# The last expert round moved into the next block, and one expert matrix fetched ahead

## The reference

```python
scores = sigmoid(x @ w_router); idx = grouped top-8 of 64 experts; wsel = 2.5 * normalised scores
routed = sum over the 8 chosen experts e of wsel[e] * (silu(x @ w_gate[e]) * (x @ w_up[e])) @ w_down[e]
x = x + g2 * (routed + swiglu(x, shared weights))
h = rmsnorm(x) * gain * (1 + scale) + shift      # the next layer's input; after layer 1: the final norm
```

## Time and profile before

| | |
|---|---|
| median of 3 runs | 1618.62 us (1614.11 to 1620.0) |
| profiled execution | 1614.77 us, its span 1613.0 us, mean TensorE clock 0.987 |
| TensorE matmuls busy | 1516.2 us, 94% of the span |
| VectorE, ScalarE, GpSimd busy | 709.3, 364.3, 94.0 us |
| moved by DMA | 580.21 MB, 360 GB/s in the mean, 420 GB/s in the expert rounds |

### The profile page before, as it was taken

How to read it: one execution, slowest core, us unless ns; L and a number is a source line. 1 busy time by engine, 2 the same in 40 slices (tenths; PEclk the granted TensorE clock), 3 DMA queues, 4 the chain that set the end, 5 groups by cost and what they waited for, 6 DMA issues and landing times. The chain is left out here.

```text
span 1613.0 us, 29632 instructions
## 1 busy us (share of the span) xinstructions
PE 1516.2 (94%) x11206; PEld 1009.5 (63%) x11206; DVE 709.3 (44%) x1980; ACT 364.3 (23%) x770; POOL 94.0 (6%) x119
## 2 busy tenths in 40 slices
PE   6999999998999999999997799999999999999986
PEld 4778765776665665565554487767566556565553
DVE  3205535215465355345454235443745534543453
ACT  3002443103111121112111244431111111211112
POOL 0000110001000000000000000001000000010000
PEclk9999999999999999999999899999999999999998
DMA  9997799339999999999999793988999999999896
GB/s 364 388 370 266 259 394 404 124 98 367 393 420 420 420 421 420 419 420 419 398 370 409 265 291 110 351 305 325 420 420 421 421 420 420 420 419 410 338 420 248
DMA packets 153578, 580.21 MB, mean 360 GB/s; under 512 B 17181, under 2 KB 62401, under 8 KB 105226
## 3 DMA queue, kind: packets, MB, share of 16 engines
q1 hardware_dynamic: 137642, 535.74, 83.8%
q0 software_dynamic: 15200, 40.92, 6.6%
q10 hardware_dynamic: 640, 2.26, 0.4%
HBM read 567.17 MB, written 26.90 MB: 368 GB/s over the span
## 5 line engine op out<-in xcount | busy, mean ns | idle before, releaser
L2431 PE MATMUL ps<-ring,scratch 128*64 128x256 f32 x3328 | 367.8, 380 | 10.0 <-DMA ring<-in_moe_w_up 8.8
L2431 PEld LDWEIGHTS ps<-ring,scratch 128*64 128x64 f32 x3328 | 245.0, 137 | 121.6 <-issue 14.3
L2497 PE MATMUL ps<-ring,scratch 128*64 128x512 f32 x896 | 200.5, 598 | 0.0
L698 PE MATMUL ps<-hT,ring 128*128 128x264 f32 x768 | 182.5, 392 | 1.3 <-ACT hT L380 1.3
L2836 DVE SCALAR_TENSOR_TENSOR scratch<-scratch,ps 128x256 f32<-128x256 f32 x62 | 29.8, 481 | 327.4 <-ACT scratch L2985 313.4
L2395 PE MATMUL ps<-scratch 128*128 128x264 bf16 x1392 | 169.6, 276 | 1.5 <-DVE scratch L2803 1.5
L698 PEld LDWEIGHTS ps<-hT,ring 128*128 128x128 f32 x768 | 147.6, 194 | 31.4 <-issue 2.8
L2395 PEld LDWEIGHTS ps<-scratch 128*128 128x128 bf16 x1392 | 121.8, 97 | 50.2 <-issue 14.3
L2803 DVE TENSOR_TENSOR scratch<-scratch,ps 128x264 f32<-128x264 f32 x240 | 102.6, 430 | 86.3 <-PE ps L2395 86.0
L2497 PEld LDWEIGHTS ps<-ring,scratch 128*64 128x64 f32 x896 | 58.1, 136 | 117.7 <-issue 86.2
L2985 ACT ACTIVATE scratch<-ps 128x256 f32<-128x256 f32 x62 | 23.8, 384 | 424.6 <-PE ps L2431 356.3
(11 more groups left out here) (402 smaller groups left out, 1458.3 us busy)
## 6 DMA issues: line engine op xcount, KB each, us to landing
ring<-in_moe_w_gate SPq DMA_DIRECT2D x128, 1024.0 KB, 20.1
ring<-in_moe_w_up SPq DMA_DIRECT2D x128, 1024.0 KB, 21.9
ring<-in_moe_w_down SPq DMA_DIRECT2D x120, 1024.0 KB, 18.0
ring<-in_ada_w SPq DMA_DIRECT2D x48, 1024.0 KB, 12.4
ring<-in_ret_w_in SPq DMA_DIRECT2D x24, 1024.0 KB, 16.7
ring<-in_state_ret SPq DMA_DIRECT2D x16, 1024.0 KB, 14.0
out_ret_sample<-ring POOLq DMA_DIRECT2D x16, 1024.0 KB, 9.2
ring<-in_gla_w_in SPq DMA_DIRECT2D x12, 1024.0 KB, 12.0
```

What stands on the lines that cost most here:

```text
L698: mm = nc.tensor.matmul(k.ps[:, bank, 0:T], w[:, c, m * P:(m + 1) * P], k.h[:, c, :], start=(c == 0), stop=(c == DC - 1))
L2431: mm = nc.tensor.matmul(k.ps[lo:lo + CAP, 2 + p, j * DE:(j + 1) * DE], xg[:, p, c, lo:lo + CAP], slot(k, n, DE)[:, c, :], start=(c == 0), ...
L2497: mm = nc.tensor.matmul(k.ps[lo:lo + CAP, 6 + half, :], hid_t[:, p, m, lo:lo + CAP], slot(k, n, D)[:, m, half * 512:(half + 1) * 512], sta ...
```

## The change

1. **Round 15 goes behind a barrier.** `experts` leaves `pe_round`, `vector_round` and `scalar_round` of round 15, with what follows them, to closures (`tail_sync`, `tail_pool`, `tail_tensor`, `tail_vector`, `tail_scalar`), which the next block (`gla` or `final`) calls first. The main block ends with round 14, with GpSimd's row fetches and with all of SyncE's loads of round 15; each engine then reads the number of extra pairs (`read_pairs`), before the barrier. Each closure holds two versions of round 15, `If(pairs > 0)` with the extra pairs and `Else` without them. The extra block is gone, and with it one barrier for each layer.
2. **`gla` starts on chunks of `h`.** Its first projection waits for each chunk of `h` rather than for a barrier. SyncE fills the ring up to `n_end + RING` before it loads `a1` and `a2`, which wait for the norm's sum.
3. **VectorE's additions move.** `acc` is added to `x` in round 14, ahead of its `hidden`; the spread of round 14's rows is then added to `x` itself by `add_last`, in place of `add_spread`.
4. **One matrix ahead.** When the order is known and the shared ups are done, SyncE loads round 1's first gate matrix into the space of `h` (`ahead`); rounds 0 and 1 are written out, and the loops begin at 2. It stands ahead of the load of round 0's last down matrix.
5. The semaphores for stored states are shared by both mixers, GLA's stale ones are cleared at its end rather than its start, and the table load at the start of `final` is no longer in ScalarE's program.

```diff
         retention(k)
-        experts(k, 0)
-        gla(k)
-        sums = experts(k, 1)
-        final(k, sums)
+        behind = experts(k, 0)
+        gla(k, behind)
+        behind = experts(k, 1)
+        final(k, behind)
...
+            behind.sync(sp)
+            sp.wait_ge(behind.norm.s_sum, 1)
             sp.dma_start(a1, inp["gla_w_a1"][0].rearrange("(c p) r -> p c r", p=P)).then_inc(s_w, 16)
...
+            behind.tensor(pe)
+
+            def project(t, m, bank, chunks=range(DC), first=False):
                 w = slot(k, loads[t], 256)
                 for c in chunks:
+                    if first:
+                        pe.wait_ge(behind.norm.s_h, c + 1)
                     mm = nc.tensor.matmul(k.ps[:, bank, 0:T], w[:, c, m * P:(m + 1) * P], k.h[:, c, :],
                                           start=(c == 0), stop=(c == DC - 1))
                 return mm
...
+            load_until(k, sp, n_sh + 3 + RING - 1)
+            sp.wait_ge(s_count, 1)
+            wait_used(k, sp, n_sh + 1)
+            wait_slot(k, sp, place(*AHEAD))
+            sp.dma_start(ahead, expert_weight(AHEAD[0], expert_at(sp, EPI + AHEAD[1])))\
+                .then_inc(k.ring_full[place(*AHEAD) % RING], 16)
             load_until(k, sp, n_sh + 3 + RING)
-            sp.wait_ge(s_count, 1)
+
...
-            with sp.Fori(1, HEAVY) as r:
+            load_round(1, ROUND[1:], PLACE)
+            with sp.Fori(2, HEAVY) as r:
...
-            k.issued = n_end
-            load_until(k, sp, n_end + KEPT)
-            for i in range(KEPT):
-                sp.wait_ge(k.ring_free[(n_end + KEPT + i) % RING], (n_end + KEPT + i) // RING)
-            sp.wait_ge(s_count, 2)
-            with sp.If(sp.value_load(number, min_val=0, max_val=XPAIRS) > 0):
-                load_extra(sp, X_LOADS, pair_experts(sp, 0))
+            read_pairs(sp, "sp")
...
+                            w = ahead if isinstance(r, int) and r == 1 and (name, e) == AHEAD else slot(k, n, DE)
                             mm = nc.tensor.matmul(k.ps[lo:lo + CAP, 2 + p, j * DE:(j + 1) * DE],
-                                                  xg[:, p, c, lo:lo + CAP], slot(k, n, DE)[:, c, :],
+                                                  xg[:, p, c, lo:lo + CAP], w[:, c, :],
...
-            with pe.Fori(1, HEAVY - 2) as r:
+            pe_round(pe, 1)
+            with pe.Fori(2, HEAVY - 2) as r:
                 pe_round(pe, r)
-            for r in range(HEAVY - 2, LAST + 1):
+            for r in range(HEAVY - 2, LAST):
                 pe_round(pe, r)
-            last_spread(pe, x_rows if layer else nxt.sum)
-            if layer:
-                for c in range(DC - 2, DC):
-                    x_rows(pe, c)
-                pe.wait_ge(s_final, 3)
-                final_small(k, pe, small)
-            else:
-                for c in range(DC - 2, DC):
-                    nxt.sum(pe, c)
-                cond_products(k, pe, k.ps[:, 4], next_group)
+            read_pairs(pe, "pe")
 
         def one_hot(v):
 
...
+            if last:
+                for c in range(DC):
+                    v.wait_ge(s_scat, DC * (r - 1) + c + 1)
+                    add_last(v, c, k.ps[:, c % 2, 0:T], DC + c).then_inc(s_add, 1)
+            elif light(r):
+                add_spread(v, r - 1)
+                v.wait_ge(s_add, DC * (r + 1))
+                for c in range(DC):
+                    ins = add_last(v, c, acc[:, c, :], c)
+                k.dve.link(v, ins)
...
+    def tail_sync(sp):
+
+        k.issued = n_end
+        load_until(k, sp, n_end + KEPT)
+        pairs = extra_pairs["sp"]
+        with sp.If(pairs > 0):
...
+        load_until(k, sp, n_end + RING)
...
+        follow = x_rows if layer else nxt.sum
+        pairs = extra_pairs["pe"]
+        with pe.If(pairs > 0):
+            pe_round(pe, LAST)
...
+        with pe.Else():
+            pe_round(pe, LAST)
+            last_spread(pe, follow)
+            for c in range(DC - 2, DC):
+                follow(pe, c)
+        if layer:
+            pe.wait_ge(s_final, 3)
+            final_small(k, pe, small).then_inc(s_final, 1)
+        else:
+            cond_products(k, pe, k.ps[:, 4], next_group)
```

More of the change, by code:

```diff
@@ L497, in __init__, with scalar @@
         self.sq, self.tmp, self.root = sq, tmp, root
[L498 to L501 removed]
+        self.s_ms, self.s_rt, self.s_prod, self.s_step, self.s_h, self.s_samples = (
+            k.sem(f"norm{layer}{which}_{n}") for n in ("meansq", "root", "scaled", "vector_step", "chunk", "samples"))
+        if not summed:
+            self.s_sq, self.s_sum = (k.sem(f"norm{layer}{which}_{n}") for n in ("squared", "summed"))
     def square(self, act, c):
         return self.k.nc.scalar.activation(self.sq[:, c, :], self.k.x[:, c, :], ACT.Square).then_inc(self.s_sq, 1)
[L507 removed]
+    def scalar(self, act, next_table=None):
         k, nc = self.k, self.k.nc
[L510 removed]
+        act.wait_ge(self.s_ms, 1)
         nc.scalar.activation(self.root, self.tmp, ACT.Sqrt).then_inc(self.s_rt, 1)
@@ L1228, with gla @@
 GLA_OUT_BANK = [0, 1, 2, 4, 5, 6, 3, 7]
-def gla(k):
+def gla(k, behind):
     nc, inp, out = k.nc, k.inp, k.out
@@ L1463, in _ @@
                     pe.wait_ge(s_qk, 2 * (t - 1))
-                project(t, 0, 2 * (t % 2))
+                if t == 0:
+                    pe.wait_ge(behind.norm.s_samples, 1)
+                project(t, 0, 2 * (t % 2), first=t == 0)
                 project(t, 1, 2 * (t % 2) + 1).then_inc(k.ring_free[loads[t] % RING], 1)
@@ L1767, in _ @@
         def _(act):
+            behind.scalar(act)
             def outers(u):
@@ L1927, in final_small, with final @@
     for c in range(DC):
-        k.nc.tensor.matmul(k.ps[0:NS, 0, 0:1], small[:, c, :], k.ones[:, 0:1], start=(c == 0), stop=(c == DC - 1))
-def final(k, sums):
+        mm = k.nc.tensor.matmul(k.ps[0:NS, 0, 0:1], small[:, c, :], k.ones[:, 0:1], start=(c == 0), stop=(c == DC - 1))
+    return mm
+def final(k, behind):
     nc, out = k.nc, k.out
@@ L2381, in last_spread @@
                                      start=True, stop=True).then_inc(s_scat, 1)
-                    if half:
-                        behind(pe, c - 2)
+                    if half and follow:
+                        follow(pe, c - 2)
         def spread(pe, r, late=0, n=PAIRS):
@@ new lines, in scalar_round, with hidden_out @@
+        def scalar_round(act, r, late=0):
+            first, last = isinstance(r, int) and r == 0, isinstance(r, int) and r == LAST
+            heavy = tiles(r) > PAIRS
+            d = done_tiles(r, late)
+            for p in range(tiles(r)):
+                if heavy and p == 0:
+                    act.wait_ge(h_done, H_GATE_UP)
+                else:
+                    n = last_of("moe_w_gate" if light(r) else "moe_w_up", r, p)
+                    act.wait_ge(k.ring_free[n % RING], r + n // RING + 1)
+                bank = 2 + p if p < PAIRS else THIRD_BANK
+                nc.scalar.activation(silu[:, p, :], k.ps[:, bank, 0:DE], ACT.Silu).then_inc(s_sil, 1)
+            if first:
+                act.wait_ge(s_ht, 1)
+            else:
+                act.wait_ge(s_scat, DC * r)
+            slots_out(act, r)
+            def hidden_out(p, bank, at=0):
+                act.wait_ge(s_hidt, d + (max(p + 1, PAIRS) if heavy else p + 1))
+                nc.scalar.copy(hid_t[:, p].rearrange("p m s -> p (m s)"), k.ps[:, bank, at:at + DE])\
+                    .then_inc(s_hidtc, 1)
+            for p in range(min(tiles(r), PAIRS)):
+                if heavy:
+                    hidden_out(p, 6, at=p * DE)
+                else:
+                    hidden_out(p, 6 + p)
+            if not last:
+                take(act, r + 1, 1, nc.scalar.copy, g_odd, late)
+            if heavy:
+                act.wait_ge(s_hid, d + 3)
+                four_slots_out(slot_token[:, PAIRS])
+            for q in range(2 * tiles(r)):
+                p, half = divmod(q, 2)
+                cols = slice(half * 512, (half + 1) * 512)
+                rows_done(act, r, p, half, d)
+                if last:
+                    nc.scalar.copy(last_rows[:, cols], k.ps[:, 6 + half, :]).then_inc(s_part, 1)
+                    continue
+                nc.scalar.copy(parts_of(p)[:, 0, cols], k.ps[:, 6 + half, :]).then_inc(s_rhi, 1)
+                if heavy and q == 1:
+                    hidden_out(PAIRS, 3)
@@ L3228, in experts @@
-    return sums
+        tail.s_sums, tail.s_final, tail.sums = k.sem(f"{tag}_final_sums"), s_final, sums
+    else:
+        tail.s_rows, tail.norm = k.sem(f"{tag}_next_mod_rows_out"), nxt
+    def tail_sync(sp):
[3 more added lines that the diff above has]
+        with sp.If(pairs > 0):
+            for i in range(KEPT):
+                sp.wait_ge(k.ring_free[(n_end + KEPT + i) % RING], (n_end + KEPT + i) // RING)
+            load_extra(sp, X_LOADS, pair_experts(sp, 0))
+            with sp.Fori(1, pairs) as i:
+                which_ = pair_experts(sp, i)
```

(6 more changed lines are left out.)

700 lines of the change are left out of this document (325 added, 375 removed).

## The result

The changed kernel takes 1640.84 us (median, 1637.39 to 1642.48), the kernel before in the same comparison 1617.43 us: ratio 1.0143, with a 95% interval of 1.0115 to 1.0171. It is slower by 23 us. The profiled execution has a span of 1640.7 us against 1613.0; that is 27.7 us, more than between the medians, because the profiled execution of before lay 2.7 us under the median of 1617.43 and that of the changed kernel 1.6 us over its own.

A forecast was written before the change was run, and what follows sets the result against it. It took TensorE (94% busy) and the weight stream as nearly balanced within the rounds. Layer 0 3.7 us slower plus layer 1 11.9 gave 15.6 us, 1630.4 from the profile, 1634 against the median; range 1623 to 1643 for eight in ten.

The forecast's parts named there:

- SyncE's last issue holds the barrier: Barrier ahead of round 15: cannot pass before SyncE's last down load issue, 877.14 and 1584.08, less 1.7 us.
- The rival in which SyncE lets go early: SyncE's eight issues take about 0.7 us each, round 15 starts 8 us earlier per layer: 1618; chance 0.12.
- Barrier and read: Ahead of round 15: one barrier and one read of the number of pairs take 1.1 us.
- The branch, 3.7 us: TensorE's jump ahead of round 15: 3.7 us, since it is farther than the earlier 3.72 us one.
- the cheap branch: Rival: the jump costs 0.33 us as in layer 1 before, 3.4 us less per layer: 1627; chance 0.17.
- The ahead load, 1.7 us in each layer: Start of the rounds: prefetched matrix makes the stream and SyncE's issues 1.7 us earlier; bounds 0 and 2.5.
- Gates and spread: Round 15, from gates to ups: 6.2 us for gates plus 5.4 for the spread with `add_last`, 11.6 us.
- Round 14 hidden later, covered: Round 14: `add_last` delays `hidden` and the rest by 1.1 us, covered by TensorE's waiting, so costing nothing.
- What comes back in layer 0, 11.6 us: GLA's start: barrier removed (8.6 us) and full clock kept (10.30 to 7.3) return 11.6 of 15.3 us.
- `a1` and `a2`, 0 with a bound of 3 us: Layer 0: small loads behind four condition and eight GLA loads arrive just when needed: 0, at most 3 us.
- more comes late: Third rival: small loads 3 us late, longer branch beside full DMA, `add_last` at upper bound: some 6 us, 1640; chance 0.13.
- as meant: Rival: barrier hides in the gate-matrix wait, both ends spared: 1604; chance 0.03, shared with SyncE early plus cheap branch.

The follow-up runs named there:

- the last variant: Changed kernel with moved down loads, early `a1`/`a2`, round 15 written once ahead of the branch, condition products and last small matmuls inside both branches: 1607.47 us, ratio 0.9960.

## Why the prediction was right, and where its terms were off

The direction and the size hold: 1640.84 us lies in the range of 1623 to 1643, 7 us above the forecast of 1634. That it is only 7 is partly luck: from profile to profile 15.6 us more were forecast and 27.7 came, so the terms missed 12 us, nearly all in one direction, and 5 of them do not show in the medians, since the profiled execution of before was a quick one and that of the changed kernel a slower one. By its steps:

- **SyncE's last issue holds the barrier: shown.** It ended at 877.91 for a predicted 875.4, and moving the eight issues away took 12.9 us off. The rival in which SyncE lets go early is out; its condition, issues of 0.7 us each, did not come (14.37 us for eight, 15.41 before).
- **Barrier and read, 1.1 us: right,** 0.96 in both layers.
- **The branch, 3.7 us: the right kind, mis-sized.** It measured 6.29 and 6.63 us, so 5.5 us more over both layers. The step is "I take 3.7", and the reason given for it, that the new jump is farther, is not what made it dear: the branch of 3.72 us ran beside an idle DMA (0.03), the new ones right behind SyncE's eight half loads, beside a full one (1.01 and 0.99), and the fetch for which each of them waits started 1.0 us behind the jump there and 3.8 us here. The prediction had this, "a branch that waits longer beside a full DMA", but only in its third rival. The Trainium skill, page "Runtime: NRT & Kernel Launch", section "Instruction fetch mechanics", gives TensorE room for 2048 instructions, from which the cheap branch was made a rival; these runs speak against that rival, since the branch in the changed kernel is not of the cheap kind in either layer. Why one branch of before took only 0.33 us no row shows. The same section says that a taken branch out of the window waits for a fetch; with that the runs agree, down to the packet in the trace and the stall moving with the jump.
- **The ahead load, 1.7 us in each layer: failed.** It measured nothing (+0.3 us, 2.4 on either side), and the waits in the full rounds are 1.3 us shorter over both layers, not 3.4. The step that failed is "from then on the stream is the slower partner, and everything that waits for it comes 1.7 us earlier". What came lies at or near its lower bound of 0.
- **Gates and spread, 11.6 us: 9.81 and 11.79.** In layer 0 the gates took 5.03 us for 6.2, and the spread 4.85 for 5.4.
- **Round 14 hidden later, covered: shown.** 1.3 us, worth nothing.
- **What comes back in layer 0, 11.6 us: 11.4.** The projection runs at the full clock in 7.36 us for 7.3. In layer 1 2.9 us for 2.6.
- **`a1` and `a2`, 0 with a bound of 3 us: mis-sized.** 2.40 us of waiting and 5.24 - 3.73 = 1.5 us of a slowed clock, 3.9 together; the run that undoes it gives 3.6. The mechanism (behind twelve loads in SyncE's queue) was named, its price was left out, and the bound did not count the clock.

The terms account for the difference of the profiled spans: 15.6 + 5.5 (branch) + 3.4 (ahead) + 3.9 (small loads) - 1.6 (gates and spread) = 26.8 of 27.7 us. What came is, in place and price, the rival "more comes late" (1640): its longer branch and its late small loads, without its dearer additions. The rival "as meant" needed SyncE away from the barrier; the runs show that it also needs the jump away from there, and `a1` early, for a gain over before: 1614.7 us without the third, 1603.1 with all three (both leave the work for extra pairs out), and 1607.5 with the jump kept but put where TensorE waits.

## What to carry to other kernels

Before work is moved across an all-engine barrier, look at what every engine still has to do ahead of it, issues of loads above all: eight issues of nearly 2 us each are work, though they compute nothing. Write the common case so that control falls through to it, and put the jump where its engine waits anyway, or where the DMA is idle; the stall, up to 6.6 us beside a full DMA and 3 to 4 beside an idle one, followed the jump wherever it was put. And when a stretch gets shorter, ask which small load, long hidden, is the next to be late: here 12 us that had been gained came back as one wait until two small loads were moved up by four places.

## What the runs showed of the hardware

- A jump on TensorE waited for one 16 KB packet of its instruction queue and went on 1.3 to 1.6 us after it had landed. Beside idle DMA engines (share 0.03) it cost 3.72 us in the kernel before and 3.05 in the last variant, beside full ones (0.99 to 1.10) 6.29 and 6.63 us in the changed kernel and 5.75 in the last variant, and there the packet started 3.1 to 3.8 us behind the jump, not 0.7 to 1.0. One branch of before took 0.33 us.
- It need not be over with the branch: 3.45 us more stood within the gates of layer 1 with the loads moved, 0.74 us in the changed kernel, and the next packet landed 1.4 and 1.2 us before TensorE went on.
- The issue of the same small load took SyncE 2.92 us behind other loads and 0.37 us after it had waited.
- 1 MB fetched ahead into idle DMA time, seen in full in the windows, changed the time by +0.3 us, with 2.4 us on either side.
